# A hybrid RWKV-7 and differential-attention decoder trunk: order of evacuations, level masks, shape of the recurrent state, first loads and ring size changed

## The reference, cut to what matters

```python
def rwkv7_step(state, inp):
    r, w, k, v, kk, a = inp
    sa = jnp.einsum('bhij,bhj->bhi', state, -kk)
    state = state * w[:, :, None, :] + sa[..., None] * (kk * a)[:, :, None, :] + v[..., None] * k[:, :, None, :]
    y = jnp.einsum('bhij,bhj->bhi', state, r)
    return state, y
...
    y = ((y - mean) * lax.rsqrt(var + GN_EPS)).reshape(B, S, RWKV_WIDTH)
    y = y.astype(p.dtype) * gn_w + gn_b
    bonus = jnp.sum(rh * kh * r_k, -1, keepdims=True) * vh
    y = (y + bonus.reshape(B, S, RWKV_WIDTH)) * g
```

## Time and profile before

| | |
|---|---|
| runs | 2014.37, 2007.73, 2006.72 us; median 2007.73 |
| profiled execution | 2012.85 us; span from first to last instruction 2011.0 us |
| TensorE busy (weight loads) | 1850.7 us (75% of the span) |
| VectorE, ScalarE, POOL busy | 1564.6, 1241.2, 116.6 us |
| HBM read | 468.15 MB |

### The profile page before, as it was taken

One profiled execution on the slowest core, in us unless ns is written; L12 is line 12 of the kernel. 1 busy time (PEld: TensorE's weight loads), 2 busy tenths in 40 slices (PEclk: granted clock), 3 DMA queues, 4 the chain that ended last, 5 costly groups with the idle time before them and its releaser, 6 DMA issues.

```text
span 2011.0 us, 31751 instructions
## 1 busy us (share of the span) xinstructions
PE 1850.7 (92%) x10552; PEld 1511.3 (75%) x10552; DVE 1564.6 (78%) x2134; ACT 1241.2 (62%) x1680; POOL 116.6 (6%) x138
## 2 busy tenths in 40 slices
PE   6968879899998886888899999999999999999998
PEld 5656667688876665776778888888888888888886
DVE  5864577565566864676599999999999999899996
ACT  4643265355555432444388877788787878878775
POOL 2011110000011011200120000000000000000000
PEclk9988799999999988899899999999999999999999
DMA  8521035266645411143499999999999999999993
GB/s 245 183 96 43 22 125 184 74 190 188 187 143 177 157 43 54 33 134 107 157 332 384 331 361 357 354 366 337 371 348 357 347 363 365 344 362 354 355 371 133
DMA packets 224510, 474.43 MB, mean 236 GB/s; under 512 B 17304, under 2 KB 42024, under 8 KB 223872
## 3 DMA queue, kind: packets, MB, share of 16 engines
q1 hardware_dynamic: 219952, 458.19, 64.7%
q0 software_dynamic: 3472, 13.65, 2.2%
q10 hardware_dynamic: 960, 1.10, 0.2%
HBM read 468.15 MB, written 1.05 MB: 233 GB/s over the span
## 4 chain that ended last, share of the span: by engine, by line
PE 79%; DVE 13%; ACT 4%; issue 2%; DMA 2%; POOL 0%; DVEq 0%; ACTq 0%; POOLq 0%
PE psum L443 22%; PE psum L445 22%; PE psum L444 22%; DVE w_lo L404 4%; PE psum L467 2%; PE psum L959 2%; ACT w_hi L391 2%; PE psum L1006 1%; DMA SH<-proj 1%; DVE SH L1563 1%; PE psum L850 1%; DVE st L1540 1%; PE psum L694 1%; DVE NB L1534 1%; ACT hN L1260 1%
## 5 line engine op out<-in xcount | busy, mean ns | idle before, releaser
L443 PE MATMUL psum<-w_hi,h_hi 128*128 128x512 f32 (+1 forms) x1776 | 715.6, 403 | 33.5 <-DVE w_lo L404 31.5
L444 PE MATMUL psum<-w_lo,h_hi 128*128 128x512 f32 (+1 forms) x1776 | 700.6, 394 | 0.0
L445 PE MATMUL psum<-w_hi,h_lo 128*128 128x512 f32 (+1 forms) x1776 | 700.4, 394 | 0.0
L443 PEld LDWEIGHTS psum<-w_hi,h_hi 128*128 128x128 f32 x1776 | 340.4, 192 | 117.1 <-DVE w_lo L404 28.3
L445 PEld LDWEIGHTS psum<-w_hi,h_lo 128*128 128x128 f32 x1776 | 340.3, 192 | 73.7
L444 PEld LDWEIGHTS psum<-w_lo,h_hi 128*128 128x128 f32 x1776 | 341.3, 192 | 67.7 <-issue 0.7
L391 ACT ACTIVATE w_hi<-ring,col 128x512 fp32r<-128x512 f32 (+1 forms) x296 | 193.0, 704 | 216.0 <-PE psum L445 206.5
L404 DVE SCALAR_TENSOR_TENSOR w_lo<-ring,col,w_hi 128x512 fp32r<-128x512 f32 (+1 forms) x296 | 216.5, 778 | 140.0 <-ACT w_hi L391 137.7
L420 DVE TENSOR_TENSOR w_lo<-ring,w_hi 128x1024 fp32r<-128x1024 f32 x144 | 172.4, 1221 | 7.6 <-ACT w_hi L416 3.2
L416 ACT ACTIVATE w_hi<-ring 128x1024 fp32r<-128x1024 f32 x144 | 151.9, 1060 | 41.0 <-PE psum L445 41.0
L420 DVE TENSOR_TENSOR w_lo<-dproj,w_hi 128x1024 fp32r<-128x1024 f32 x120 | 145.9, 1223 | 17.3 <-ACT w_hi L416 13.7
(11 more groups left out here) (319 smaller groups left out, 2334.6 us busy)
## 6 DMA issues: line engine op xcount, KB each, us to landing
ring<-in_expert_w_gu SPq DMA_DIRECT2D x128, 512.0 KB, 5.4
SH<-in_expert_w_gu SPq DMA_DIRECT2D x120, 512.0 KB, 5.9
proj<-in_expert_w_gu SPq DMA_DIRECT2D x104, 512.0 KB, 6.1
dproj<-in_expert_w_gu SPq DMA_DIRECT2D x72, 512.0 KB, 6.0
dproj<-in_expert_w_down SPq DMA_DIRECT2D x72, 512.0 KB, 5.1
ring<-in_expert_w_down SPq DMA_DIRECT2D x64, 512.0 KB, 5.0
ring<-in_in_proj SPq DMA_DIRECT2D x48, 512.0 KB, 4.5
ring<-in_dense_w_gu SPq DMA_DIRECT2D x88, 256.0 KB, 3.1
```

The lines of the kernel that those rows point to most:

```text
L443: pe.matmul(o, h[0], w[0], start=start, stop=False, skip_group_check=True)
L444: pe.matmul(o, h[0], w[1], start=False, stop=False, skip_group_check=True)
L445: return pe.matmul(o, h[1], w[0], start=False, stop=stop, skip_group_check=True)
```

## The change

- The copies out of PSUM in the solve and in the state's update take `more = -NS`. The splits that stood ahead of them follow after them (`ahead(..., -1)`), up to the second block beyond those taken.
- The level masks are no longer multiplied into the matrices by POOL. They are loaded (into `hT`), transposed by TensorE (`lower`) and copied by VectorE once, and multiplied in when VectorE copies `X` out.
- The state is held as 128x64 for each pair of heads (even head in partitions 0 to 63, odd in 64 to 127), `keep` is gone, and the products for it run as 64x64 tiles. `sa` and the state's part of `y` (`y1`) take two banks each. The chunk's own part of `y` (`y2`) is made for both chunks after them, and VectorE adds it.
- POOL's steps at the end are VectorE's: `gate_fold` within the levels, `gated` after the group norm. One side step of VectorE stands ahead of `Z`'s subtraction now, where both stood behind it.
- ScalarE's copy of the first values and the memory's squares move from ahead of `U` into levels 0 and 1 of the first tile.
- For layer 0 `mu` and the first half of `vec` are issued right behind the lora weights; the squares' unused outputs go to `NB`.
- The ring has five slots before the experts. The experts' ring keeps its 14 (`W1` is no slot of it any more).
- The scores of the two maps of a head are issued alternately.

```diff
-RING, BLK = 4, 1024
+RING, BLK = 5, 1024
...
-        state = sb("state", [P, 4, P])
-        keep = sb("keep", [P, 4, P])
+        state = sb("state", [P, 4, HD])
...
+                    transposes(("lower", 0), [hT[:, i * P:(i + 1) * P] for i in range(4)])
+                    transposes(("lower", 1), [hT[:, 4 * P:5 * P]])
...
-                                    last = pe.matmul(halves(o, b2), Cm[cs, lv, h, :], half_cols(Tm[cs, h, :], b2, 0), start=True, stop=True)
+                                    last = pe.matmul(halves(o, b2), mats[cs, h, 0, :], half_cols(Tm[cs, h, :], b2, 0), start=True, stop=True)
                                 else:
-                                    last = pe.matmul(o, C4[cs, h, :], Tm[cs, h, :], start=True, stop=True)
+                                    last = pe.matmul(o, mats[cs, h, 0, :], Tm[cs, h, :], start=True, stop=True)
...
-                        bank = open_work(("sa", l, t, p))
-                        for b in range(4):
-                            last = pe.matmul(bank[tk, b * P:(b + 1) * P], aiT[:, b, tk], state[:, b, :], start=True, stop=True)
-                        B.filled(last, ("sa", l, t, p))
-                        bank, ybank = open_work(("s", l, t, p)), open_work(("y", l, t, p))
-                        for b in range(4):
-                            cs = slice(b * P, (b + 1) * P)
-                            pe.matmul(ybank[tk, cs], arT[:, b, 1, tk], state[:, b, :], start=(b == 0), stop=False, skip_group_check=True)
-                        for b in range(4):
-                            cs = slice(b * P, (b + 1) * P)
-                            pe.matmul(bank[:, cs], nb(ENC)[tk, t, cs], pv[tk, t, 2 * RW + b * P:2 * RW + (b + 1) * P],
-                                      start=(b == 0), stop=False, skip_group_check=True)
-                        pe.wait_ge(sa_ready, n + 1)
-                        for b in range(4):
-                            cs = slice(b * P, (b + 1) * P)
-                            last = pe.matmul(bank[:, cs], nb(B_)[tk, t, cs], SA[tk, cs], start=False, stop=(b == 3), skip_group_check=True)
-                        B.filled(last, ("s", l, t, p))
-                        for h in range(8):
-                            hs = slice(h * HD, (h + 1) * HD)
-                            pe.matmul(ybank[tk, hs], mats[tk, h, 3, :], pv[tk, t, 2 * RW + h * HD:2 * RW + (h + 1) * HD],
-                                      start=False, stop=False, skip_group_check=True)
-                            last = pe.matmul(ybank[tk, hs], mats[tk, h, 1, :], SA[tk, hs], start=False, stop=(h == 7), skip_group_check=True)
-                        B.filled(last, ("y", l, t, p))
+                        for name, of in (("sa", aiT), ("y1", arT[:, :, 1, :])):
+                            banks = [open_work((name, l, t, p, par)) for par in range(2)]
+                            for b in range(4):
+                                for par in range(2):
+                                    r = side_of(par)
+                                    last = pe.matmul(banks[par][tk, b * HD:(b + 1) * HD], of[r, b, tk], state[r, b, :], start=True, stop=True)
+                                    if b == 3:
+                                        B.filled(last, (name, l, t, p, par))
+                        bank = open_work(("s", l, t, p))
+
+                        def add_to_state(rows_, values, first):
+                            for b in range(4):
+                                for par in range(2):
+                                    hs = slice((2 * b + par) * HD, (2 * b + par + 1) * HD)
+                                    last = pe.matmul(bank[side_of(par), b * HD:(b + 1) * HD], rows_[:, hs], values[:, hs],
+                                                     start=first and b == 0, stop=not first and b == 3, skip_group_check=True)
+                            return last
+                        add_to_state(nb(ENC)[tk, t, :], pv[tk, t, 2 * RW:3 * RW], True)
+                        for par in range(2):
+                            B.wait_evacuated(pe, ("sa", l, t, p, par))
+                        B.filled(add_to_state(nb(B_)[tk, t, :], SA[tk, :], False), ("s", l, t, p))
                         if p == 0 and t == 0:
                             some(kv, 1)
...
+                    banks = [open_work(("y2", l, t, c)) for c in range(2)]
+                    for h in range(8):
+                        hs = slice(h * HD, (h + 1) * HD)
+                        for c in range(2):
+                            cs = side_of(c)
+                            pe.matmul(banks[c][cs, hs], mats[cs, h, 3, :], pv[cs, t, 2 * RW + h * HD:2 * RW + (h + 1) * HD],
+                                      start=(h == 0), stop=False, skip_group_check=True)
+                        for c in range(2):
+                            cs = side_of(c)
+                            last = pe.matmul(banks[c][cs, hs], mats[cs, h, 1, :], SA[cs, hs], start=False, stop=(h == 7), skip_group_check=True)
+                            if h == 7:
+                                B.filled(last, ("y2", l, t, c))
...
+                    sp.dma_start(hT[:, 0:5 * P], consts[:, LEVELS]).then_inc(small_in, 16)
...
+                if l == 0:
+                    pool.dma_start(mu, mus[0].partition_broadcast(P)).then_inc(mu_in, 16)
...
-                pool.wait_ge(sq_done, 2 * 3 * l + TT)
-                pool.dma_start(mu, mus[l].partition_broadcast(P)).then_inc(mu_in, 16)
+                if l:
+                    pool.wait_ge(sq_done, 2 * 3 * l + TT)
+                    pool.dma_start(mu, mus[l].partition_broadcast(P)).then_inc(mu_in, 16)
...
-                    for lv in range(5):
-                        m = M("lvl")[:, lv:lv + 1, :]
-                        pool.tensor_tensor(Cm[:, lv, :, :] if lv < 4 else C4, mats[:, :, 0, :], bc(m, 8, CH), MUL).then_inc(c_ready, 1)
...
-                        wts = sm[:, 0:16].rearrange("p (t b c) -> p t b c", t=TT, b=4)[:, t, :, p:p + 1]
-                        pool.tensor_tensor(keep[:, :, :], bc(C("bd").unsqueeze(1), 4, P), bc(wts, 4, P), MUL).then_inc(keep_ready, 1)
...
+                        copy(U_[side_of(c), :], ("U", l, t, c), lambda b, c=c: b[side_of(c), :], scale=-1.0, more=-NS)
+                    ahead(("U", l, t, 1), -1)
                     for lv in range(5):
-                        copy(hT[:, 512:1024], ("TT", l, t, lv))
+                        copy(hT[:, 512:1024], ("TT", l, t, lv), more=-NS)
+                        ahead(("TT", l, t, lv), -1)
+                        if l == 0 and t == 0 and lv == 0:
+                            act.activation(v_first[:, :, :], pv[:, :, 2 * RW:3 * RW], ACT.Copy).then_inc(v_kept, 1)
+                        if l == 0 and t == 0 and lv == 1:
+                            act.wait_ge(mem_in_s, 16)
+                            for mt in range(TT):
+                                if mt:
+                                    act.wait_ge(msq_done, mt)
...
+                        for par in range(2):
...
+                    for i, (v0, v1) in enumerate(((0, 4), (4, 5))):
+                        bank = B.wait_filled(dve, ("lower", i))
+                        for c in range(2):
+                            of = bank[side_of(c), 0:(v1 - v0) * P].rearrange("p (v t) -> p v t", t=P)
+                            ins = dve.tensor_copy(lower[side_of(c), v0:v1, :], of[:, :, side_of(c)])
...
+                def gate_fold():
+
+                    add, gate_v = nb(A_), nb(G_)
+                    tt(add.rearrange("p t (n c) -> p t n c", c=HD), v_v.rearrange("p t (n c) -> p t n c", c=HD), bc(sm[:, 16:32].rearrange("p (t n) -> p t n", t=TT).unsqueeze(3), TT, RH, HD), MUL)
+                    yield
+                    tt(add, add, bc(V("gn_b").unsqueeze(1), TT, RW), ADD)
+                    yield
+                    for t in range(TT):
+                        B.wait_evacuated(dve, ("gup", l, t))
+                    tt(add, add, gate_v, MUL)
+                    yield
+                    tt(gate_v, gate_v, bc(V("gn_w").unsqueeze(1), TT, RW), MUL)
+
+                def gated(t):
+
+                    for par in range(2):
+                        B.wait_filled(dve, ("y1", l, 1, 1, par))
+                    y = nb(EC)[:, t, :]
+                    tt(y, y, nb(G_)[:, t, :], MUL)
+                    ins = dve.tensor_tensor(hNv[:, t, 0:RW], y, nb(A_)[:, t, :], ADD)
+                    if t:
+                        ins.then_inc(ycat_rw, 1)
                 gn_steps = [group_norm(t) for t in range(TT)]
+                extra = chain(qk_norm(), gate_fold())
+
...
+                def side_step(t):
+                    if next(extra, "end") == "end" and t:
+                        next(gn_steps[0], None)
...
+                        below = half_cols(lower[:, lv, :], b2, 0) if lv < 4 else lower[:, 4:5, :]
                         for c in range(2):
                             name = ("X", l, t, lv, c)
```

(48 more changed lines are left out.)

120 lines of the change are left out of this document (42 added, 78 removed).

## The result

The changed kernel takes 1980.22 us in the median of four runs (1979.57 to 1988.44), the kernel before beside it 2007.22 (2005.98 to 2014.37). The ratio is 0.987, with a 95% interval from 0.983 to 0.990: faster, by 27 us of medians, which is less than 2%. The two profiled executions stand further apart, 2012.85 and 1979.57, 33.3 us, and so do their spans, 2011.0 and 1977.7; the reading goes by these. The forecast was a saving of 44.4. Nearly all of the saving lies in the two recurrences, and the experts' stretch is as long as it was.

The account below looks back on a forecast made before the run. Recurrences were taken as bound by latency between engines, the state's update by TensorE, the experts as an unmoved TensorE wall. Savings 11.6 + 23.8 + 12 + 1 - 4 = 44.4 us take the median 2007.73 to 1963.3 us, range 1940 to 1988.

Parts of the forecast that it names:

- Masking of m12: Recurrence, ahead of m3: its copies no longer stand behind splits, TensorE's waits go; 11.6 us saved (8 to 12).
- Copies of X: Solve levels: X copied ahead of splits, so most of TensorE's 37.7 us of waits go; 23.8 us saved.
- the split then fits beside it: Tile 1 levels: with copies done during TensorE's half block, the split fits there too; 3.45 us saved per split level.
- Rival (b): Levels: split and side step before Z's subtraction make VectorE the bound; 16 us plus attention's 10; 1985 us, chance 0.20.
- The clock, rival (a): Recurrences: with gaps gone, TensorE runs more at full clock; 15 us more saved, 1948 us, chance 0.15.
- State: State's update: smaller products alternating between array tiles; 3.0 us per tile, 12 us saved (4 to 21).
- the Trainium skill's rule: State's update: different array tiles execute weight loads and matmuls in parallel, so this part would gain some 20 us.
- Rival (c): State's update: waits on banks, 1.5 us for each chunk, take all 12 us saved; 1975 us, chance 0.06.
- Start: Kernel start: shifted rows 3 us earlier, against 2 us for the lower transposes and copies; net 1 us saved.
- Attention: Mainly attention: VectorE takes over POOL's steps and adds y2; net cost 4 us (0 to 10).
- (d): Levels: idle time only moves to the next block, only start and state change; about 2003 us, chance 0.05.
- (e): Recurrences and attentions: splits come late, 2.75 us per block; with all 28, 33 us slower, 2040 us, chance 0.06.

Follow-up runs that it names:

- the seven profiles: Profiles of the changed kernel (two) and five follow-up kernels whose code in the levels is the same; their levels take 145.8 to 156.4 us.
- The kernel with the order alone: Kernel before, with only the changed order of VectorE's and ScalarE's work in the recurrence; masks, state, start and ring stay: 1989.14 us, ratio 0.989.

## Why the prediction was right in direction and 11 to 17 us off in size

The forecast was a saving of 44.4 us. The profiled executions give 33.3, the medians 27.0 (29.4 for the changed kernel measured again). The parts below are those of the profiled executions.

**Masking of m12: 11.6 forecast, 8.6 measured.** The long waits went, for the reason given. The step that was mis-sized took the whole wait ahead of `m3`, while 0.78 us of it, the last bank's own masking, is left in each of the four tiles (1.6 us in each layer's list above). 4 x 0.78 = 3.1 is the difference. All later kernels repeat 4.5 us for this stage to within 0.2.

**Copies of X: 23.8 forecast, 9.7 measured. This is the step that failed**, at "the split then fits beside it". (Its other term, that a side step ahead of the subtraction hides some of `Z`, held in layer 0's tile 0, whose levels fell from 40.0 to 35.7 us.) In the levels TensorE was idle 162.1 - 116.1 = 46.0 us before, and the waits for `X`'s copy (37.7) and the subtraction (8.2) account for it. After, the idle time is 152.4 - 110.7 = 41.7: 6.3 + 27.1 for the same two, 6.7 for low parts and 1.7 for ScalarE's copy of TT. So 31.4 us of waits went and 27.1 took their place, one step further on. In this profile the fall in idle time is 4.3 us, and the other 5.4 are TensorE's busy time, mostly of layer 0's tile 1 at a higher clock. The second profile has 155.3 - 117.5 = 37.8 of idle time, 8.2 less than before, and 1.4 more of busy time. Even the best of the seven profiles gains 16 us here, so the miss of the 23.8 is not a matter of the profile. The forecast looked at whether `Z` could start, and priced what stands between copy and subtraction for the odd levels of layer 1 only. Rival (b) had the mechanism and 16 us of price for it, against 18.9 measured at the subtraction (27.1 - 8.2; in the second profile 24.3 - 8.2 = 16.1). Its case as a whole (1985, with the attention's 10 us) did not come.

**The clock, rival (a)**, went both ways in the first profile: up in layer 0's tile 1, down in layer 1's (0.82 to 0.65). The forecast had no case in which it falls. But it is not the change alone that decides it. Within the levels of layer 1's tile 1 the clock was 0.77 before, 0.62 in both profiles of the changed kernel, and 0.84 or 0.85 in four kernels with the same levels; in layer 0's tile 1 the changed kernel itself took 36.7 us at 0.87 and 39.6 at 0.70. The kernel with the order alone waited as long for the subtraction, 29.4 us, at 0.82 to 0.86 in all four tiles. What decides the clock is not settled. The rival's price of 15 us does not follow from its own terms either: a third of its 33 us, done at twice the clock, saves 5.5 in each layer.

**State: 12 forecast, 16.4 measured**, 14.0 of it not by the order of the copies. Kernels with the same code in these stages take 60.5 to 64.6 us there, so both numbers can be off by up to 3 us. The record in tiles that share a side was taken between 34 and 62 ns; it is 32, below the lower bound. Against the 14.0 the forecast's 12 is nearer than the 20 us reckoned by the Trainium skill's rule. New waits stand at `y1` in the first chunk of every tile, 0.54 to 0.77 us, and in one second chunk 0.28 at `y1` and 0.64 at `s`: 3.5 us in all, where 0.5 for each tile, 2 in all, was allowed. Rival (c), the banks, is refuted at its 1.5 us a chunk: the pressure that the Trainium skill (TensorEngine Tiling (Array Packing), Gotcha 1: PSUM Pressure) names costs under 1 us in each chunk here. Exchanging the orders gives 3.6 + 5.5 = 9.1 us back, so alternation carries over half of the 14.0; what the narrower products of `sa`, `y1` and `s` gave by themselves was not tried alone.

**Start: +1 forecast, +0.5 measured**, within what two profiles of one start differ by. The move of `mu` is worth about 3, as taken. The `lower` transposes and their copies cost about what they were given, but the idle time at 37.60 stayed 6.39 us, not near 4 as forecast. Why it did was not tried.

**Attention: -4 forecast, -3.2 in layer 0 and +1.2 after layer 1's recurrence.** From the first score to the last product with the values layer 0 takes 50.6 us against 47.5 before, layer 1 46.1 against 47.1, in both profiles of the changed kernel. VectorE is busy for 45.55 us of layer 0's window, against 41.85. TensorE's wait for `attend` of the changed kernel in layer 0, against the earlier trace rows, grew by 1.2:

```profile
PE psum L805 <- DVE SH L1919: 10.8, 3, 6.4
```

The forecast took the 471 ns of the earlier trace rows for the price of a tiny operation beside GpSimd. It is a mean of four: three took 220 or 221 ns, and one 1223. The timeline of before shows that one; the second view is of the changed kernel, where GpSimd does nothing there:

```profile
250.55 1.26 POOL L1193 TENSOR_TENSOR NB<-NB,vec 128x512 f32<-128x512 f32 x1
250.60 1.22 DVE L1540 SCALAR_TENSOR_TENSOR st<-st 128x2 f32<-128x2 f32 x1
```

```profile
L1523 DVE SCALAR_TENSOR_TENSOR st<-st 128x2 f32<-128x2 f32 x4 | 0.9, 222 | 0.1
```

VectorE's operation begins 0.05 us after GpSimd's and ends with it. Just before, at 249.43, another tiny one of VectorE takes 1.06 us beside a GpSimd operation of 1.04 (elsewhere 0.17). So these two cost 1.9 us in layer 0, about the forecast's "some 2 us", which came from the wrong row by luck.

**Rivals (d) and (e).** The idle time moved in the levels only, and not all of it, so (d) is half true where it matters and wrong for the whole. (e) is there in small: four late low parts, 6.7 us, always early in tile 1, and in every kernel above that has the changed splits in the state's update. The kernel with the order alone leaves these as they were and has none; putting only these splits back ahead was not tried. The rival counted 16 blocks in the recurrences and 12 in the attentions; the trace of before has 18 and 18 (36 of L443 in each of these stages of a layer, four to a block).

## What to carry to other kernels

When a wait in a chain over several engines is removed by moving work behind it, the work lands in front of the next link; price that link before counting the wait as gained, level by level, and put optional work where its engine has the longest gap in that very stage. In a chain that leaves TensorE idle for over a quarter of the time a total can hide what an edit does, since the clock gives or takes more than the edit: compare stage boundaries and the engine's busy time for the same products, and profile the same kernel twice, or compare several kernels with the same code in that stage, before believing a few microseconds. Small products in different tiles of the array should alternate, one by one, even if the tiles share rows or columns.

## What was unexpected of the hardware

The same 408 records of one tile's levels took TensorE 30.0 us at a granted clock of 0.62 and 21.5 at 0.91. The two kernels differ in the order of VectorE's work, but four more with the first one's order there took 22.4 to 22.9 us at 0.84 or 0.85, so the order is not what sets it alone. One record of a 64x64 product costs 32 ns if the tile of the array changes with every product, 38 if it changes with every fourth, and 58 in one tile over 32 records. An operation of VectorE on 128x2 that took 0.22 us otherwise took 1.22 when it began beside a GpSimd operation of 1.26 us, and ended with it.
